# Low parts of u tiles 8 to 45 on VectorE between the parts of the decoding, in a transformer layer with a PEER feed-forward

## The reference

```python
s = jnp.einsum('thcd,hcnd->thcn', qb, sub_keys)        # scores of 128 keys, two sets, 8 heads
s_top, i_top = lax.top_k(s, 16)
cand = s_top[:, :, 0, :, None] + s_top[:, :, 1, None, :]
best, pos = lax.top_k(cand.reshape(..., 256), 16)
eidx = jnp.take_along_axis(cand_idx, pos, axis=-1)
g = jax.nn.softmax(best, axis=-1)
h = jax.nn.gelu(jnp.einsum('td,thkd->thk', xb, jnp.take(u, eidx, axis=0)))
out = jnp.einsum('thk,thkd->td', g * h, jnp.take(v, eidx, axis=0))
```

## Time and profile before

| | before |
|---|---|
| median of 3 runs | 1603.5 us |
| profiled run, its own time | 1601.73 us |
| its span | 1599.9 us |
| TensorE matmul busy | 1578.9 us (99%) |
| VectorE busy | 1276.5 us (80%) |
| ScalarE busy | 630.1 us (39%) |
| GpSimd busy | 533.3 us (33%) |
| HBM traffic | 266 GB/s over the span |

### The profile page before, as it was taken

The page is one execution under the profiler, slowest core; times in us unless marked ns, Lnnn a source line. Parts: engine busy times, 40 slices in busy tenths (PEclk is TensorE's granted clock), DMA queues, the critical chain, the costliest instruction groups (busy, mean ns, idle before and its releaser), DMA issues.

```text
span 1599.9 us, 24488 instructions
## 1 busy us (share of the span) xinstructions
PE 1578.9 (99%) x9566; PEld 1393.4 (87%) x9566; DVE 1276.5 (80%) x2390; ACT 630.1 (39%) x996; POOL 533.3 (33%) x261
## 2 busy tenths in 40 slices
PE   9999999999999999999999999999999999999998
PEld 7897977888989999989999998888878888888886
DVE  3024366345899999999998879999989999999997
ACT  5424345532222333445555333333334433434332
POOL 4433223351235789421010233333332232232200
PEclk9999999999999999999999999999999999999999
DMA  5332212135123669699998899999999999999972
GB/s 202 143 145 80 70 54 80 60 108 175 53 93 121 181 185 319 217 332 319 354 341 280 290 418 405 405 414 409 405 388 422 417 410 411 394 389 420 405 286 76
DMA packets 141633, 427.05 MB, mean 267 GB/s; under 512 B 11344, under 2 KB 73040, under 8 KB 120272
## 3 DMA queue, kind: packets, MB, share of 16 engines
q1 hardware_dynamic: 118224, 274.47, 47.5%
q0 software_dynamic: 23296, 151.04, 23.5%
HBM read 378.77 MB, written 46.14 MB: 266 GB/s over the span
## 4 chain that ended last, share of the span: by engine, by line
PE 62%; DVE 29%; DMA 4%; issue 3%; ACT 1%; POOL 0%; SPq 0%; DVEq 0%; ACTq 0%
PE bank L1437 19%; PE bank L1438 18%; PE bank L1439 18%; DVE acc L1311 4%; DVE uvb L1273 4%; DVE wlo L1265 3%; PE bank L1743 3%; DMA raw<-in_u 3%; DVE idx L1179 1%; DVE idx L1171 1%; DVE val L1170 1%; DVE val L1178 1%; DVE tmp L1172 1%; DVE cand L1214 1%; DMA raw<-in_uv 1%
## 5 line engine op out<-in xcount | busy, mean ns | idle before, releaser
L1437 PE MATMUL bank<-xhi,whi 128*128 128x352 f32 (+1 forms) x1408 | 488.5, 347 | 5.0 <-ACT hout L917 2.8
L1438 PE MATMUL bank<-xlo,whi 128*128 128x352 f32 (+1 forms) x1408 | 481.1, 342 | 0.0
L1439 PE MATMUL bank<-xhi,wlo 128*128 128x352 f32 (+1 forms) x1408 | 480.7, 341 | 0.0
L714 POOL DMA_INDIRECT uvb<-in_uv,eidx x128 | 212.1, 1657 | 551.5 <-DVE acc L1311 400.7
L896 ACT ACTIVATE whi<-raw 128x1024 fp32r<-128x1024 f32 x255 | 268.8, 1055 | 202.7 <-PE bank L1439 133.9
L1265 DVE TENSOR_TENSOR wlo<-raw,whi 128x1024 fp32r<-128x1024 f32 x215 | 262.6, 1222 | 52.9 <-ACT whi L896 52.6
L1437 PE MATMUL bank<-whi,ahi 128*128 128x512 f32 x762 | 300.1, 394 | 2.0 <-DVE wlo L1265 2.0
L1439 PE MATMUL bank<-whi,alo 128*128 128x512 f32 x762 | 297.4, 390 | 0.0
L1438 PE MATMUL bank<-wlo,ahi 128*128 128x512 f32 x762 | 297.2, 390 | 0.0
L1437 PEld LDWEIGHTS bank<-xhi,whi 128*128 128x128 f32 x1408 | 265.1, 188 | 22.2 <-DVE wlo L1265 4.4
L1439 PEld LDWEIGHTS bank<-xhi,wlo 128*128 128x128 f32 x1408 | 265.6, 189 | 15.4
(11 more groups left out here) (225 smaller groups left out, 1858.8 us busy)
## 6 DMA issues: line engine op xcount, KB each, us to landing
raw<-in_u SPq DMA_DIRECT2D x128, 512.0 KB, 6.5
raw<-in_uv SPq DMA_DIRECT2D x127, 512.0 KB, 9.7
g_scratch<-stage SPq DMA_DIRECT2D x48, 512.0 KB, 6.8
gl<-g_scratch SPq DMA_DIRECT2D x32, 768.0 KB, 8.7
raw<-in_w_in SPq DMA_DIRECT2D x22, 1024.0 KB, 4.8
h_scratch<-hout SPq DMA_DIRECT2D x96, 192.0 KB, 5.4
hl<-h_scratch SPq DMA_DIRECT2D x24, 768.0 KB, 11.5
raw<-in_w_q SPq DMA_DIRECT2D x6, 1024.0 KB, 4.8
```

What stands on the lines that cost most here:

```text
L714: nc.gpsimd.indirect_dma_start(out=uvb[:, r % UVB, :], out_offset=None, in_=a["uv"][:, :], in_offset=bass.IndirectOffsetOnAxis(ap=eidx[:, ...
L1437: mm(out, lh, rh, start=first, stop=False)
L1438: mm(out, lh, rl, start=False, stop=False)
L1439: return mm(out, ll, rh, start=False, stop=last)
```

## The change

VectorE makes the low parts of u tiles 8 to 45 itself, between the parts of the selections by a table, `LOWS_IN`; GpSimd makes those of tiles 0 to 7 only and has no part in a tile from then on. Its first five `gather_u` now wait for the high parts of tiles 28, 31, 34, 37 and 40 (`GATHER_HI` + 3j). All step numbers behind the decoding move up: the exponential 39 to 43, the weights 43 to 46, transposes 42 to 46, copies 46 to 50, one-hots 48 to 51, first and second g load 95 and 99 to 98 and 102, the first four sum steps from 89, 91, 93, 95 to 92, 93, 94, 95; the later ones stay.

```diff
@@ -86,21 +86,26 @@
 FUSED = NT - FIRST_FUSED
 LAG = 4
 LAST = 5
-POOL_ONLY = 40
-EXP_STEP = 39
-NORM_STEP = 43
-PICKS_TILE = 42
-PICKS_STEP = 46
-HOT0, HOT1, HOT2 = 48, 86, 90
-C_STEPS = [41, 42, 43, 44, 45, 47] + [49 + 3 * i for i in range(NCP - 6)]
-C_TILE, C_STEP = 80, 80
+POOL_ONLY = 8
+LOWS_IN = {0: (8, 9, 10), 1: (11,), 2: (12, 13), 3: (14, 15), 4: (16, 17), 5: (18,), 6: (19,), 7: (20,), 8: (21, 22), 9: (23, 24),
...
+           19: (38,), 20: (39, 40), 21: (41, 42), 22: (43, 44), 23: (45,)}
+DVE_FIRST = 46
+assert [s for k in sorted(LOWS_IN) for s in LOWS_IN[k]] == list(range(POOL_ONLY, DVE_FIRST))
+EXP_STEP = 43
+NORM_STEP = 46
+PICKS_TILE = 46
+PICKS_STEP = 50
+HOT0, HOT1, HOT2 = 51, 89, 93
+C_STEPS = [46, 47, 48, 49, 50, 51] + [53 + 3 * i for i in range(NCP - 6)]
+C_TILE, C_STEP = 83, 83
 HOT_LEAD = 2
-GL_FIRST, GL_SECOND = 95, 99
+GL_FIRST, GL_SECOND = 98, 102
 LN2_STEP = 225
 FIRST_NORM = (248, 249, 250, 252)
-GATHER_TILE = 25
+GATHER_HI = 29
 SEL_PARTS = 6
-SUM_STEPS = [89, 91, 93, 95] + [97 + i * 59 // 29 for i in range(29)] + [156 + i * 94 // 31 for i in range(31)]
+SUM_STEPS = [92, 93, 94, 95] + [97 + i * 59 // 29 for i in range(29)] + [156 + i * 94 // 31 for i in range(31)]
 assert len(SUM_STEPS) == len(set(SUM_STEPS)) == NG // 2
 
 
@@ -717,14 +722,13 @@
 
             for s in range(POOL_ONLY):
                 tile_low(s)
-                if s == GATHER_TILE:
-                    pool.wait_ge(cidx_done, 1)
-                    for g in range(CG):
-                        nc.gpsimd.dma_start(cidx4[g * CT:(g + 1) * CT, :], cidx[CP:P, g * CT:(g + 1) * CT]).then_inc(cidx_in, 16)
-                if s == GATHER_TILE + 1:
-                    pool.wait_ge(cidx_in, 16 * CG)
-                if GATHER_TILE < s <= GATHER_TILE + UVB:
-                    gather_u(s - GATHER_TILE - 1)
+            pool.wait_ge(cidx_done, 1)
+            for g in range(CG):
+                nc.gpsimd.dma_start(cidx4[g * CT:(g + 1) * CT, :], cidx[CP:P, g * CT:(g + 1) * CT]).then_inc(cidx_in, 16)
+            pool.wait_ge(cidx_in, 16 * CG)
+            for j in range(UVB):
+                pool.wait_ge(tile_hi, GATHER_HI + 3 * j)
+                gather_u(j)
             for j in range(UVB, NCP):
                 gather_u(j)
             pool.wait_ge(idx_done, 1)
@@ -1384,11 +1388,13 @@
             for n, c in enumerate(SEL_ORDER):
                 for part in range(SEL_PARTS):
                     select(n, c, part)
+                    for s in LOWS_IN.get(SEL_PARTS * n + part, ()):
+                        tile_low(s)
                 if n == 0:
                     V.scalar_tensor_tensor(cidx[:, :], picks[:, 0, c, :], float(P), picks[:, 1, c, :], ALU.mult, ALU.add).then_inc(cidx_done, 1)
                 if c == 0:
                     V.scalar_tensor_tensor(eidx[:, :], picks[:, 0, 0, :], float(P), picks[:, 1, 0, :], ALU.mult, ALU.add).then_inc(idx_done, 1)
-            for s in range(POOL_ONLY, 2 * NT):
+            for s in range(DVE_FIRST, 2 * NT):
                 tile_low(s)
                 if s - 1 in SUM_STEPS:
                     sums(SUM_STEPS.index(s - 1))
```

More of the change, by code:

```diff
@@ L88 @@
 LAST = 5
-POOL_ONLY = 40
-EXP_STEP = 39
-NORM_STEP = 43
-PICKS_TILE = 42
-PICKS_STEP = 46
-HOT0, HOT1, HOT2 = 48, 86, 90
-C_STEPS = [41, 42, 43, 44, 45, 47] + [49 + 3 * i for i in range(NCP - 6)]
-C_TILE, C_STEP = 80, 80
+POOL_ONLY = 8
+LOWS_IN = {0: (8, 9, 10), 1: (11,), 2: (12, 13), 3: (14, 15), 4: (16, 17), 5: (18,), 6: (19,), 7: (20,), 8: (21, 22), 9: (23, 24),
+           10: (25, 26), 11: (27,), 12: (28,), 13: (29,), 14: (30, 31), 15: (32, 33), 16: (34, 35), 17: (36,), 18: (37,),
+           19: (38,), 20: (39, 40), 21: (41, 42), 22: (43, 44), 23: (45,)}
[8 more added lines that the diff above has]
+C_TILE, C_STEP = 83, 83
 HOT_LEAD = 2
-GL_FIRST, GL_SECOND = 95, 99
+GL_FIRST, GL_SECOND = 98, 102
 LN2_STEP = 225
 FIRST_NORM = (248, 249, 250, 252)
-GATHER_TILE = 25
+GATHER_HI = 29
 SEL_PARTS = 6
-SUM_STEPS = [89, 91, 93, 95] + [97 + i * 59 // 29 for i in range(29)] + [156 + i * 94 // 31 for i in range(31)]
+SUM_STEPS = [92, 93, 94, 95] + [97 + i * 59 // 29 for i in range(29)] + [156 + i * 94 // 31 for i in range(31)]
 assert len(SUM_STEPS) == len(set(SUM_STEPS)) == NG // 2
```

## The result

The kernel after takes 1608.24 us (median of 20 runs, 1604.93 to 1614.2), the kernel before in the same comparisons 1603.97 (20 runs, 1600.41 to 1609.29). The ratio is 1.0026, 95% interval 1.0017 to 1.0035: slower by 4.3 us, a little over the 0.2% that I named. Forecast were 1605.4 with 1598.0 to 1609.5. The sign and the range hold, the size is 4.3 us where I had 1.9.

The account below looks back on a forecast made before the run. TensorE bound first, DMA from 898.5 to 970.1, then VectorE, and TensorE after the fused steps. With 1.9 us gained by tile 52 included, step 105 came +1.9 us, taking the median from 1603.5 to 1605.4; range 1598.0 to 1609.5.

Parts of the forecast that it names:

- The decoding: Four selections with 38 low parts on VectorE: 144.4 us, ending at 674.3, costing TensorE nothing.
- Rival C: Long decoding operations aren't GpSimd's doing: decoding ends at 705.4, low parts up to 30 us late, near 1635; chance 0.03.
- The wait for one-hots: TensorE's first g quads, near 702, wait for both one-hot batches: a loss of 4.9 to 5.2 us.
- a loss of 7.1 us into one of 5.2: TensorE's lost time up to the first g quads falls, gaining 1.9 us by tile 52.
- What starts the one-hots: Exponential behind tile 43 ready at about 677.7, VectorE there at 677.8; the one-hots were then dated from the decoding's end.
- The queues: First sum to step 105, DMA-paced: first sum 9.7 us later, 2.2 MB less of 27.6, +1.9 us at step 105.
- the middle between the bounds: Start of step 105's low part taken between 969.3 and 974.6: +1.9 us against 970.1.
- the fast bound: Queues filled at once behind the first sum, as step-on-step sums free ring slots faster: step 105 at 969.3, 0.8 earlier.
- the slow bound: Slow first 10.5 us behind the first sum kept: step 105 at 974.6, 4.5 us later than 970.1.
- That delay stays: From 970 on VectorE binds with unchanged work to the fused end, then TensorE, so the +1.9 us reaches the end.
- A: Queues absorb the crowding behind the last g stores: step 105 at 964.8, 5.3 us early, 1598.2; chance 0.26.
- B: g loads too late for the products of steps 100 and 104: up to 7.5 us each, 1613.2; chance 0.25.

Follow-up runs that it names:

- e5: The kernel before with the first two g loads in steps 98 and 102 instead of 95 and 99; 1607.4 us, ratio 1.0017.
- e10: The kernel before with dots_c spread, two fewer ahead of the first one-hots, and first four sums at 81, 84, 87, 90; 1597.5 us, ratio 0.9951.
- e1: The changed kernel with the first four sum steps back at 89, 91, 93, 95; 1604.48 us, ratio 1.0005 to the kernel before.
- e8: The changed kernel's step numbers and later u gathers, with low parts as before (GpSimd tiles 0 to 39, VectorE from 40); 1607.4 us, ratio 1.0016.
- e3: The changed kernel with the last four g stores one per step in 92 to 95, instead of two in 92 and two in 93; 1610.7 us, ratio 1.005.
- e9: The changed kernel with dots_c spread, two fewer ahead of the one-hots, and first four sums at 84, 87, 90, 93; 1594.06 us, ratio 0.9939.
- e13: The changed kernel with only the dots_c spread, two fewer ahead of the one-hots, sums still at 92 to 95; 1604.04 us, ratio 0.999.
- e6: The changed kernel with the sixth dots_c in step 52 instead of 51 and first four sums at 84, 87, 90, 93; 1598.32 us, ratio 0.9958.
- e12: e9 with the exponential behind tile 42 and two more pairs of sums early (82, 84, 87, 90, 93, 95); 1596.64 us, ratio 0.9947.
- e11: e8 with the spread dots_c and the first four sums at 84, 87, 90, 93, as in e9; 1596.06 us, ratio 0.9943.
- e2: The changed kernel with the sixth dots_c in step 52 instead of 51; 1606.82 us, ratio 1.0018 to the kernel before.

## Why the prediction came out as it did

**The decoding: right.** Forecast 144.4 us and an end at 674.3, measured 141.6 and 671.5; the first low part forecast to be done at 533.8, measured from 532.61 on, 1.2 us each (behind part 0 stand three of them); L1235 at 1.23 in all four; u tiles at an even distance up to tile 49 but for the transposes (4.83 us once), and no wait of TensorE among them. They came 3.84 apart (689.57, 693.41, 697.25 behind the last three) where before had 3.867. That isn't the change's doing: tiles 0 to 28 take 107.52 us in after, but also in e5 and e10 with before's code, and 108.26 in e1 with after's. Rival C is gone. The Trainium skill (SBUF — State Buffer, Who interferes with whom) says that VectorE and GpSimd share a pair of ports which one of them holds at a time; the trace agrees: the 3.32 and 13.32 of the earlier trace rows are gone with GpSimd's subtractions, and in e8, which has them back, all four of that multiplication take 3.3 us.

**The wait for one-hots: right in its length, but not in its price.** Forecast 4.9 to 5.2 us, measured 4.9; the second batch forecast ready at 704.7, measured 703.12 + 0.69 = 703.8. What I hadn't priced is TensorE's clock behind the wait, 2.5 us. Tile 52 was forecast at 719.4 and stands at 721.19. Before stood at 724.22, of which three batches (2.9 us) are only done later now: the gain is 0.1 us and not 1.9 (between single traces: e1 and e3, with after's code up to here, stand at 721.91 and 720.65, e5 with before's at 727.26). The step that failed is the sentence that turned a loss of 7.1 us into one of 5.2, as if only the waiting time counted. Rows 2 showed 3.7 us in three waits of at most 1.5 without a loss of clock; the forecast wait turned out as one of 4.2 and one of 0.7. The Trainium skill (TensorE: Matmul & The Clock Gate, HAM oscillation — how this bites in real kernels) describes matmuls that start at the lower clock behind a wait for data; 0.50 in after and 1.00 in e9 agree.

**What starts the one-hots: half right.** I had the end of the decoding and the exponential arrive together, and worked on from the first. It is the exponential, by 1.6 us. e8 shows that this isn't a detail: without the move of the low parts, with the decoding over some 15 us earlier, nothing changes that can be measured. The term that I worked out from the decoding's end had no hold on the time, and that the wait came out right from it is luck: the two ends lay only 1.6 us apart.

**The queues: the mechanism right, the middle between the bounds wrong.** Step 105 was forecast at 972.0, with 969.3 and 974.6 as bounds, and stands at 976.89, 4.9 later. Three terms make that up:
- The first sum came at 909.69, 11.5 us later than the 898.16 of before, and not 9.7: the gain that was missing above, 1.8 us.
- The slow 10.5 us were kept: 206 GB/s behind the first sum, as before 208. I had taken the middle, which is 2.65 us too little. The reason that I gave for the fast bound (sums step on step free slots faster) is not what the trace shows: with its ring full, GpSimd hands out the next gather only behind the first sum in both kernels, and the slow start is the same. A filled start does exist, in e1, but with the sums spread as in before; I had taken for a matter of the sums' spacing what goes with the other transfers under way.
- The rest ran at 409 GB/s and not 416, 0.8 us for 23 MB, less a little for fewer bytes (66.9 us x 377 = 25.2 MB against 25.4).

1.8 + 2.65 + 0.4 is 4.85, and e8, whose step 105 stands at 976.85, says that this isn't one execution's chance. With the right start the slow bound would have given 976.4.

**The end.** "That delay stays" held up to the noise: after is 6.8 us late at step 105 and 8.4 at step 155 and at the end. e8, with the same step 105, takes 206.85 us from there to step 155 and after 208.96, before 207.30, so that 1.7 us are of that one execution. The traces then say +6.8, the medians +4.3; the profiled run of before was a quick one (above). By the medians the terms can't be settled one by one, only in groups: e13 gives 4.2 us (5.8 by the ratios) for wait and clock, e1 3.8 for the place of the sums; they aren't shares of the 4.3, since e13 improves on before too at its place (waits of 2.6 us in all, before 3.7).

**Rivals.** A (step 105 near 965) did not occur in after, but e6 and e9 make it: with sums from step 84 the crowding is indeed absorbed. B's wait is real (e5, e12) but absent in after. B's sum had 10.8 us from a g load's issue to its product, and the traces have 9.0 (after): 15.6 less 9.0 is e5's 6.6. In after the raw loads come late instead, which I hadn't among the rivals: one took 17.9 us to arrive, and one was held back with SyncE for 14.31 us. The earlier trace rows had announced this with 5.52.

**What stays open.** Whether the low parts on VectorE are worth anything at all: after against e8 (1.0026 and 1.0016) and e9 against e11 (0.9939 and 0.9943) differ by 1.6 and 0.6 us with intervals of 1.4 to 2.6 us on each side, so that a gain or loss of 2 to 3 us could hide there. Nor does e8 part the numbers from the later gathers of u rows; before with these gathers alone wasn't run. Why two waits of 1.9 and 1.5 us in e2 lose clock and 1.3 and 1.5 in before don't wasn't tried.

## What to carry to other kernels

When work moves between engines and the step numbers behind it move too, try the kernel without the moved work first: here it was as slow as the whole change, and the moved work itself was covered. Where a queue is full for a long stretch, look at its start: begin the transfers that need it while it has room, in ones and twos, rather than when their results are due; here this was worth 6 to 10 us, more than the change. And a wait of TensorE costs more than its length once the clock falls behind it; splitting it in two didn't save that here (e2), shortening it to 1.2 and 1.4 us did (e9, e13).

## What the runs showed of the hardware

- Behind one wait of 4.21 us TensorE ran at a granted clock of 0.50 from 701 to about 709, with matmuls at 0.49 us instead of 0.32: 2.5 us on top of the wait.
- With the queues full (share 1.02, 409 GB/s), the hand-out of two DMAs held SyncE for 14.31 us, and with their order changed that of one load for 12.00 (e3); most other hand-outs in the same stretch take 0.33 to 0.5. A load of 512 KB handed out by 918.42 was used only 17.9 us later.
- Behind the first sum the queues of before and after move 206 to 208 GB/s for 10.5 us (some 60 in the first 5 us) before they reach 409 to 421; in e1, where g stores are under way at that moment, they run at 314 to 393 at once.
- With GpSimd's subtractions beside it a VectorE multiplication takes 3.3 us (before, e8), without them 1.23 (after).
- Moving 32 subtractions off GpSimd and 38 into VectorE's decoding raised VectorE's busy time by 4.9 us only.
